# Gated rows finished in their own turn, and two down tiles side by side in PSUM, in the feed-forwards of a two-block network

## The chip, the cores and the metric

One core of a Trainium2 chip runs the whole network in one launch. The metric is the device time in microseconds (us) of one execution. "PE" is TensorE, "DVE" VectorE, "ACT" ScalarE, "POOL" GpSimd and "SP" the queue that issues the weight transfers.

## What is computed

A network of two blocks on 512 positions of width 1024. What matters here are the two convolutional feed-forwards at the end of the second block (`l` = 0 and 1). In outline:

```
y = rmsnorm(h, ffn_norm_g[l])
u = y @ w_up[l]                      # 1024 -> 2 x 2816
u = causal conv of width 3 over positions, per channel, plus bias
g = silu(u[:, :2816]) * u[:, 2816:]  # the gated rows
h = h + g @ w_down[l]                # 2816 -> 1024
```

Everything is kept transposed: a tile has 128 channels on the partitions and the 512 positions along the free axis. Float32 products are made of three TensorE products: each operand is split into a high part of reduced precision and the remainder, and high*high, high*low and low*high are summed in PSUM.

## The kernel before

**Plan.** `Plan` (from line 90) lists every PSUM tile of the program in the order in which TensorE fills them. A tile has 1024 float32 columns; there are four such buffers (`BANKS2`), and each tile takes the next one in the ring, waiting until the tile that was there has been read (`before`, `free`). The plan also lists the 128x128 weight blocks in the order of use, eight to a unit (`UT`).

**Weights.** SP loads a unit from memory into one of five `raw` buffers (line 417). ACT copies it to its high part `whi` (line 814), POOL subtracts to get `wlo` (line 1194); there are three buffers of each. ACT does this inside its own stream: `psum(key)` of ACT (line 818) converts whatever units the plan allows before and, in the feed-forwards, right after the wait for tile `key`. A unit may be converted once the last tile that used the unit three before it is finished.

**Feed-forward** (`ffn`, in `Plan`, and in TensorE's, ACT's and DVE's streams). The 2816 gated channels are made in two halves (`f` = 0, 1) of `FH` = 11 rows of 128 channels. For each row there is one *up tile*: 16 weight blocks, 8 into each 512-column half (the two inputs of the gate), so 48 matmuls. After the 11 up tiles of a half come 8 *down tiles* (`m` = 0 to 7), each 11 weight blocks over the 11 gated rows, so 33 matmuls. With two layers and two halves there are four passages from up tiles to down tiles.

A gated row is made so, once its up tile is finished:

- DVE multiplies the tile by `rstd` (`scaled`, line 1210, 1024 columns);
- ACT writes tap 0 and the bias for each half into `cv` (line 831, twice);
- DVE adds the other two taps to each half (line 1216, four instructions);
- ACT takes Silu of the first half into `tmp` (line 831);
- DVE multiplies it by the second half into `hf` (line 1210);
- ACT copies `hf` to the high part `Fhi` (`high`, line 831);
- DVE subtracts to get `Flo` (`low`, line 1210).

The order is written out by hand. In turn `r` DVE does the scaling and the taps of row `r`, and after that the product of row `r-1`; a `Flo` is only made when a third `hf` is asked for (`to_split`, two buffers) or at the end (`flush`). ACT does tap 0 of row `r`, then Silu of row `r-1`, then the high part of row `r-2`. So a row is spread over three turns. TensorE's `linear` waits before block `k` of a down tile for the `Flo` of row `k` (semaphore `lo`).

After a down tile DVE adds it to `X` (`resid`). For the second half of layer 0 this is done inside `feed`, which also makes the next stage's operand.

Of the kernel before, what the change touches and what calls it, by code (L numbers as in the profile page):

```python
# [90 lines left out]
class Plan:  # L91
# [3 lines left out]
    def __init__(self):  # L95
# [2 lines left out]
        self.last = {}  # L98
        self.slot, self.before, self.in_slot, self.turn = [], [], {}, 0

        def tile(key, free, weights=(), again=None, slots=None):
            self.index[key] = n = len(self.free)
            self.free.append(free)
            slot = (slots or range(BANKS2))[self.turn % len(slots or range(BANKS2))]
            self.turn += 1
            self.slot.append(slot)
            self.before.append(self.in_slot.get(slot))
            self.in_slot[slot] = n
            start = len(self.split)
            if again is not None:  # L110
                start, weights_n = self.first[self.index[again]], self.count[self.index[again]]
            else:
                weights_n = len(weights)
                for w in weights:
                    if len(self.split) % UT == 0:
                        self.units.append(("split", len(self.split) // UT))
                    self.split.append(w)
            self.first.append(start)
            self.count.append(weights_n)
            for i in range(start, start + weights_n):  # L120
                self.last[("split", i // UT)] = len(self.free) - 1
# [131 lines left out]
        def ffn(l):  # L253
            for f in range(2):
                for j in range(FH):
                    tile(("up", l, f, j), [("conv", 4 * ((2 * l + f) * FH + j + 1))],
                         ktiles(f"up{l}", f * FH + j) + ktiles(f"up{l}", 2 * FH + f * FH + j))
                    if f == j == 0:
                        norm(f"ffn{l}")
                for m in range(8):  # L260
                    tile(("dn", l, f, m), [("resid", RAT[f"f{l}{f}"] + m + 1)],
                         [(f"dn{l}", f * FH + k, m) for k in range(FH)])

        ffn(0)
        for m in range(8):
# [40 lines left out]
def hf_of(j):  # L306

    return HAT[f"act{j // (2 * FH)}{j // FH % 2}"] + j % FH + 1


def build(nc, a):
# [23 lines left out]
    with ctx:  # L335
# [62 lines left out]
        def v_(name, i=0, n=1):  # L398
            return vec[:, VAT[name][0] + i:VAT[name][0] + i + n]
# [25 lines left out]
        def _(pe):  # L425
# [326 lines left out]
            def ffn(l):  # L752
                for f in range(2):
                    for j in range(FH):
                        tile(("up", l, f, j))
                        for part in range(2):
                            last = linear(("up", l, f, j), *((Ahi, Alo) if l else (Bhi, Blo)), 0, SAT[f"ffn{l}"] + 1, XO, offset=KD * part,
                                          ks=list(range(KD)), col0=T * part)
                        done(last)
                        if f == j == 0:  # L760
                            norm(f"ffn{l}")
                    for m in range(8):
                        tile(("dn", l, f, m))
                        done(linear(("dn", l, f, m), Fhi, Flo, 0, SAT[f"act{l}{f}"] + 1, XO))

# [20 lines left out]
        def _(ac):  # L786
# [308 lines left out]

            def ffn(l):
                for f in range(2):
                    for r in range(FH + 2):
                        if r < FH:
                            ps = psum(("up", l, f, r))  # L1100
                            if f == r == 0:
                                root(f"ffn{l}")
                            j = (2 * l + f) * FH + r
                            if j >= 3:
                                ac.wait_ge(sem("hf"), hf_of(j - 3))
                            ac.wait_ge(sem("scaled"), j + 1)
                            for part in range(2):
                                c = (part * 2 + f) * FH + r
                                act(cv[:, j % 3, part, :], ps[:, part * T:(part + 1) * T], ACT.Identity,
                                    v_(f"ffn_b{l}", c), v_(f"ffn_w{l}", 88 + c), "ca")  # L1110
                        if 1 <= r <= FH:
                            j = (2 * l + f) * FH + r - 1
                            ac.wait_ge(sem("conv"), 4 * j + 4)
                            act(tmp[:, j % 2, 0:T], cv[:, j % 3, 0, :], ACT.Silu, sem_name="se")
                        if r >= 2:
                            high(Fhi[:, r - 2, :])
                    if f == 0:
                        for m in range(8):
                            psum(("dn", l, f, m))
# [85 lines left out]
        def _(ve):  # L1205
# [3 lines left out]
            def tt(out, x, y, op, s=None):  # L1209
                do(TTi(out, x, y, op), s)  # L1210
# [174 lines left out]
            out(PAIRS - 1, TN - 1)  # L1385
            scales(1)

            def resid(key, m, gate=None, n_sem="resid"):
                ps = psum(key)
                if gate is None:  # L1390
                    tt(X[:, m, :], ps[:, 0:T], X[:, m, :], ADD, n_sem)
                else:
                    stt(X[:, m, :], ps[:, 0:T], gate, X[:, m, :], MUL, ADD, n_sem)

# [249 lines left out]
            def feed(name, gain, end, hi, lo):  # L1644

                i = NI[name]
                ve.wait_ge(sem("psum"), plan.index[("ss", NORMS[i - 1][0])] + 1)

                def ahead(k):
                    ve.wait_ge(sem("ah"), LAT[name] + k + 1)  # L1650
                    stt(lo[:, k, 0:T], X[:, k, :], v_(gain, k), hi[:, k, 0:T].bitcast(fp32), MUL, SUB, "lo")
                    if k:
                        ve.wait_ge(sem("n_sq"), nsq[0] + k + 1)
                        g = NK[i] + k
                        first = sq[:, (g - 1) % 3, 0:T] if k == 1 else acc[:, 0:T]
                        tt(acc[:, 0:T], first, sq[:, g % 3, 0:T], ADD, "n_acc")

                for m in range(8):
                    resid((*end, m), m)
                    if m:  # L1660
                        ahead(m - 1)
                ahead(7)
                nsq[0] += 8

            def used():
                ts(small2[:, 0:1], eps1[:, 0:1], 1.0, None, MUL, s="n_use")
# [6 lines left out]

            def ffn(l):
                for f in range(2):
                    for r_ in range(FH + 1):
                        if r_ < FH:

                            ps = psum(("up", l, f, r_))
                            j = (2 * l + f) * FH + r_  # L1680
                            if f == r_ == 0:
                                ve.wait_ge(sem("n_rs"), 2 * NI[f"ffn{l}"] + 2)
                            scaled(ps, "scaled")
                            if f == 1 and r_ == FH - 1:
                                used()
                            for part in range(2):
                                ve.wait_ge(sem("ca"), 2 * j + part + 1)
                                c = (part * 2 + f) * FH + r_
                                for back in (1, 2):
                                    y = cv[:, j % 3, part, back:T]  # L1690
                                    stt(y, ps[:, part * T:part * T + T - back], v_(f"ffn_w{l}", 44 * (2 - back) + c), y,
                                        MUL, ADD, "conv")
                        if r_:
                            j = (2 * l + f) * FH + r_ - 1
                            ve.wait_ge(sem("se"), j + 1)
                            e = tmp[:, j % 2, 0:T]
                            b = to_split(T)
                            tt(b, e, cv[:, j % 3, 1, :], MUL, "hf")
                            queued(Fhi[:, r_ - 1, :], Flo[:, r_ - 1, :])
                    flush()  # L1700
                    if f == 0:
                        for m in range(8):
                            resid(("dn", l, f, m), m)

            feed("ffn0", "ffn_g0", ("ev",), Bhi, Blo)
            ffn(0)
# [21 lines left out]
            flush()  # L1728
            feed("ffn1", "ffn_g1", ("od",), Ahi, Alo)
            ffn(1)  # L1730
            for m in range(8):
                resid(("dn", 1, 1, m), m)
            sums("f2")
            ve.wait_ge(sem("n_rs"), 2 * NI["f2"] + 2)
            for k in range(KD):
# [121 lines left out]
```

## Time and profile before

| | us |
|---|---|
| median of 3 runs | 2248.68 |
| lowest and highest | 2245.04, 2254.93 |
| the profiled execution's own time | 2256.99 |
| its span in the trace | 2254.8 |
| mean granted TensorE clock | 0.926 of full speed |

The profile is of one execution, 8.3 us above the median of the runs. Spans and starts in its rows are in us from the start of the span, unless marked ns. The feed-forwards and the short convolution mixer between them fill the stretch from about 1293 to 2236 us.

### The profile page before, as it was taken

The page shows a single profiled execution, that of the slowest core. Times are in us where ns is not written, and L with a number is a line of the kernel's source. Part 1 is how long each engine was busy: PE and PEld are TensorE (multiplying, and loading weights), DVE is VectorE, ACT ScalarE, POOL GpSimd, SP SyncE. Part 2 cuts the span into 40 slices and gives each one's busy share as a digit, 9 for nine tenths or more (in the row PEclk, how much of TensorE's full clock was granted, in tenths as well). Part 3 has the DMA queues.
Part 4 walks back from the last instruction along what each step waited for, and adds up shares of the span by engine and source line. Part 5 has one row for each costly group of instructions (what it writes and reads, how often), then busy time and mean ns, then how long its engine had stood idle before and what let it go on. Part 6 is the DMA issues. An engine that isn't in the chain of part 4 may idle for free.

```text
span 2254.8 us, 27585 instructions
## 1 busy us (share of the span) xinstructions
PE 1992.5 (88%) x10708; PEld 1606.3 (71%) x10708; DVE 1171.8 (52%) x1657; ACT 887.4 (39%) x1199; POOL 694.8 (31%) x310
## 2 busy tenths in 40 slices
PE   4899999999787977976683999999999999999996
PEld 3687677777666867764472788788778877878875
DVE  2422666664276757657799334225444464522442
ACT  3252656654334453443331444234432234422432
POOL 1121011102214223222235344344344443444432
PEclk6799999999978989878796999999999999999998
DMA  7111211212211100112120222223223322323331
GB/s 277 38 56 54 76 48 67 76 67 85 59 37 37 39 29 29 38 52 80 37 76 10 84 84 94 88 96 98 84 87 101 93 89 90 94 84 94 94 94 47
DMA packets 46257, 166.80 MB, mean 74 GB/s; under 512 B 5392, under 2 KB 5520, under 8 KB 45872
## 3 DMA queue, kind: packets, MB, share of 16 engines
q1 hardware_dynamic: 44208, 158.88, 22.1%
q10 hardware_dynamic: 1920, 6.16, 0.8%
q8 instruction: 86, 1.41, 0.3%
q14 instruction: 43, 0.35, 0.1%
HBM read 162.92 MB, written 2.10 MB: 73 GB/s over the span
## 4 chain that ended last, share of the span: by engine, by line
PE 75%; DVE 17%; ACT 4%; issue 2%; DMA 1%; POOL 0%; ACTq 0%; DVEq 0%
PE ps L454 20%; PE ps L455 20%; PE ps L456 20%; PE ps L559 4%; PE ps L572 2%; PE ps L589 2%; DVE ex L1210 2%; DVE sq L1210 2%; DVE hf L1210 2%; ACT sq L831 1%; DVE tmp L1210 1%; PE ps L488 1%; DVE acc L1210 1%; PE ps L476 1%; DVE wS L1605 1%
## 5 line engine op out<-in xcount | busy, mean ns | idle before, releaser
L1194 POOL TENSOR_TENSOR wlo<-raw,whi 128x1024 fp32r<-128x1024 f32 x251 | 607.7, 2434 | 1303.8 <-ACT whi L814 1303.8
L814 ACT ACTIVATE whi<-raw 128x1024 fp32r<-128x1024 f32 x251 | 257.7, 1055 | 669.1 <-PE ps L456 647.2
L454 PE MATMUL ps<-Ahi,whi 128*128 128x512 f32 (+1 forms) x784 | 320.1, 408 | 27.5 <-issue 11.9
L455 PE MATMUL ps<-Alo,whi 128*128 128x512 f32 (+1 forms) x784 | 314.9, 402 | 0.0
L456 PE MATMUL ps<-Ahi,wlo 128*128 128x512 f32 (+1 forms) x784 | 313.5, 400 | 0.0
L1210 DVE TENSOR_TENSOR ps<-ps,rstd 128x1024 f32<-128x1024 f32 (+1 forms) x60 | 69.7, 1162 | 263.8 <-PE ps L456 227.3
L454 PEld LDWEIGHTS ps<-Ahi,whi 128*128 128x128 f32 x784 | 154.8, 197 | 72.5 <-issue 23.0
L454 PE MATMUL ps<-Fhi,whi 128*128 128x512 f32 x416 | 167.5, 403 | 13.1 <-DVE Flo L1210 12.9
L456 PEld LDWEIGHTS ps<-Ahi,wlo 128*128 128x128 f32 x784 | 154.6, 197 | 33.7
L455 PEld LDWEIGHTS ps<-Alo,whi 128*128 128x128 f32 x784 | 154.9, 198 | 32.1 <-issue 0.5
L1216 DVE SCALAR_TENSOR_TENSOR cv<-ps,vec,cv 128x511 f32<-128x511 f32 (+1 forms) x176 | 131.9, 749 | 71.6 <-ACT cv L831 66.9
L456 PE MATMUL ps<-Fhi,wlo 128*128 128x512 f32 x416 | 165.9, 399 | 0.0
L455 PE MATMUL ps<-Flo,whi 128*128 128x512 f32 x416 | 165.6, 398 | 0.0
L1210 DVE TENSOR_TENSOR X<-ps,X 128x512 f32<-128x512 f32 x48 | 33.2, 692 | 211.4 <-PE ps L456 211.4
L455 PE MATMUL ps<-Blo,whi 128*128 128x512 f32 x352 | 139.2, 395 | 0.0
L454 PE MATMUL ps<-Bhi,whi 128*128 128x512 f32 x352 | 139.2, 395 | 0.0
L456 PE MATMUL ps<-Bhi,wlo 128*128 128x512 f32 x352 | 138.2, 393 | 0.0
L559 PE MATMUL ps<-K,Q 128*128 128x256 f32 (+1 forms) x320 | 115.0, 474 | 2.2 <-ACT V L831 1.2
L454 PEld LDWEIGHTS ps<-Fhi,whi 128*128 128x128 f32 x416 | 79.4, 191 | 37.8 <-DVE Flo L1210 20.7
L831 ACT ACTIVATE sq<-sq,small 128x768 f32<-128x768 f32 (+1 forms) x96 | 76.2, 794 | 72.5 <-DVE small L1349 72.3
L454 PE MATMUL ps<-Hhi,whi 128*128 128x512 f32 x224 | 80.8, 361 | 14.6 <-issue 9.0
L456 PEld LDWEIGHTS ps<-Fhi,wlo 128*128 128x128 f32 x416 | 79.6, 191 | 17.7
(252 smaller groups left out, 3919.9 us busy)
## 6 DMA issues: line engine op xcount, KB each, us to landing
raw<-in_units SPq DMA_DIRECT2D x299, 512.0 KB, 3.7
X<-in_xT ACTq DMA_DIRECT2D x1, 2048.0 KB, 12.8
out_xT<-X SPq DMA_DIRECT2D x8, 256.0 KB, 2.1
CX<-in_ctxT ACTq DMA_DIRECT2D x1, 1024.0 KB, 15.7
masks<-in_masks ACTq DMA_DIRECT2D x1, 512.0 KB, 3.5
acc<-in_rope ACTq DMA_DIRECT2D x1, 384.0 KB, 3.0
gmw<-in_gmw ACTq DMA_DIRECT2D x1, 384.0 KB, 2.9
bs<-in_bs ACTq DMA_DIRECT2D x1, 384.0 KB, 3.5
```

The costliest lines, as they stand in the source:

```text
L454: nc.tensor.matmul(out, sh, mh, start=first, stop=False)
L455: nc.tensor.matmul(out, sh, ml, start=False, stop=False)
L456: return nc.tensor.matmul(out, sl, mh, start=False, stop=last)
L476: last = nc.tensor.matmul(ps[:, c0:min(n, c0 + T)], ones[:, 0:P], acc[:, c0:min(n, c0 + T)], start=True, stop=True)
L559: last = nc.tensor.matmul(ps[:, o0:o0 + c1 - c0], Q[:, p % 2, i, q * P:(q + 1) * P], K[:, p % 2, i, c0:c1], start=True, stop=True)
L572: last = nc.tensor.matmul(ps[64 * i:64 * i + 64, 0:P], V[:, t, h * HV:(h + 1) * HV], PT[:, i, n * P:(n + 1) * P], start=n == 0, stop=n == ...
L589: last = nc.tensor.transpose(ps[:, n * P:(n + 1) * P], Pr[:, u % 3, n * P:(n + 1) * P], ident[:, :])
L814: nc.scalar.activation(whi[:, s % CONV, :], raw[:, c % RAW, :], ACT.Copy).then_inc(sem("whi"), 1)
L831: do(nc.scalar.activation(out, in_, f, scale=scale, **kw), sem_name)
L1194: nc.gpsimd.tensor_tensor(wlo[:, s % CONV, :], raw[:, plan.unit_at[("split", s)] % RAW, :], whi[:, s % CONV, :].bitcast(fp32), ALU.subtrac ...
L1210: do(TTi(out, x, y, op), s)
L1216: do(STTi(out, x, sc, y, op0, op1), s)
```

## The change

In ACT's and DVE's streams, a row is finished in the turn of its own up tile: ACT does tap 0, waits for the two taps of the first half (not for all four), takes Silu, waits for the product and makes the high part; DVE does scaling and taps, waits for Silu, multiplies, waits for the high part and makes `Flo`.

In the plan and in TensorE's stream, down tiles 0 and 1 share one PSUM buffer, tile 0 in its first 512 columns and tile 1 in its last. TensorE does the blocks of rows 0 to 9 for `m` = 0, those of rows 0 to 9 for `m` = 1, and then row 10 for `m` = 0 and for `m` = 1. The first signal comes after 10 blocks, the second after 12 more; both additions to `X` wait for the second. The weight blocks are stored in this new order. The number of matmuls is the same.

```diff
-        def tile(key, free, weights=(), again=None, slots=None):
+        def tile(key, free, weights=(), again=None, slots=None, beside=None):
...
+            else:
+                slot = self.slot[self.index[beside]]
+                self.before.append(None)
...
+                w = lambda m, ks: [(f"dn{l}", f * FH + k, m) for k in ks]
+                tile(("dn", l, f, 0), [("resid", RAT[f"f{l}{f}"] + 2)], w(0, range(FH - 1)))
+                tile(("dn", l, f, 1), [("resid", RAT[f"f{l}{f}"] + 2)],
+                     w(1, range(FH - 1)) + w(0, [FH - 1]) + w(1, [FH - 1]), beside=("dn", l, f, 0))
+                for m in range(2, 8):
+                    tile(("dn", l, f, m), [("resid", RAT[f"f{l}{f}"] + m + 1)], w(m, range(FH)))
...
-                    for m in range(8):
+                    for m in range(2):
+                        ps = tile(("dn", l, f, m))
+                        for i in range(FH - 1 + 2 * m):
+                            k, o = (i, m) if i < FH - 1 else (FH - 1, i - FH + 1)
+                            pe.wait_ge(sem("lo"), SAT[f"act{l}{f}"] + k + 1)
+                            last = product(ps[:, o * T:(o + 1) * T], tuple(weights(("dn", l, f, m), i)),
+                                           (Fhi[:, k, :], Flo[:, k, :]), k == 0, k == FH - 1)
+                        done(last)
+                    for m in range(2, 8):
...
-                        if 1 <= r <= FH:
-                            j = (2 * l + f) * FH + r - 1
-                            ac.wait_ge(sem("conv"), 4 * j + 4)
-                            act(tmp[:, j % 2, 0:T], cv[:, j % 3, 0, :], ACT.Silu, sem_name="se")
-                        if r >= 2:
-                            high(Fhi[:, r - 2, :])
+                        ac.wait_ge(sem("conv"), 4 * j + 2)
+                        act(tmp[:, j % 2, 0:T], cv[:, j % 3, 0, :], ACT.Silu, sem_name="se")
+                        high(Fhi[:, r, :])
...
-                        if r_:
-                            j = (2 * l + f) * FH + r_ - 1
-                            ve.wait_ge(sem("se"), j + 1)
-                            e = tmp[:, j % 2, 0:T]
-                            b = to_split(T)
-                            tt(b, e, cv[:, j % 3, 1, :], MUL, "hf")
-                            queued(Fhi[:, r_ - 1, :], Flo[:, r_ - 1, :])
-                    flush()
+                        ve.wait_ge(sem("se"), j + 1)
+                        b = to_split(T)
+                        tt(b, tmp[:, j % 2, 0:T], cv[:, j % 3, 1, :], MUL, "hf")
+                        queued(Fhi[:, r_, :], Flo[:, r_, :])
+                        flush()
```

## Rows read from the trace of the kernel before

**Rows 1.** The page, busy time of engines: us, share of span, instructions.
```profile
PE 1992.5 (88%) x10708; PEld 1606.3 (71%) x10708; DVE 1171.8 (52%) x1657; ACT 887.4 (39%) x1199; POOL 694.8 (31%) x310
PE 75%; DVE 17%; ACT 4%; issue 2%; DMA 1%; POOL 0%; ACTq 0%; DVEq 0%
```

**Rows 2.** Waits of PE, 1245 to 2255 us: in total, times, longest.
```profile
PE ps L454 <- DVE Flo L1210: 12.9, 10, 2.8
```

**Rows 3.** The same view, 1790 to 1830 us (mixer's output tiles).
```profile
PE ps L454 <- DVE Flo L1210: 2.8, 1, 2.8
```

**Rows 4.** Windows by stage, up and down in turn: length, busy by engine, PEclk, DMA.
```profile
1305.09:1417.50 112.41, 112.41 (x483) 90.89 (x481) 53.39 (x66) 49.15 (x61) 47.77 (x20) 1.00 0.30 94
1417.50:1482.80 65.30, 62.78 (x265) 50.23 (x264) 13.23 (x18) 15.95 (x18) 26.31 (x11) 0.97 0.29 89
1482.80:1603.66 120.86, 120.86 (x530) 99.16 (x529) 54.06 (x67) 47.28 (x59) 52.61 (x22) 1.00 0.30 96
1603.66:1668.34 64.68, 62.71 (x266) 50.27 (x264) 33.04 (x30) 23.40 (x30) 27.23 (x11) 0.97 0.30 90
1872.42:1982.70 110.28, 110.28 (x482) 90.31 (x481) 53.38 (x66) 49.09 (x61) 47.85 (x20) 1.00 0.31 96
1982.70:2048.05 65.35, 62.39 (x265) 49.55 (x264) 13.23 (x18) 15.93 (x18) 26.27 (x11) 1.00 0.28 89
2048.05:2171.25 123.20, 123.20 (x529) 99.79 (x528) 54.06 (x67) 47.33 (x59) 52.56 (x22) 1.00 0.32 94
2171.25:2235.58 64.33, 61.47 (x265) 49.09 (x263) 13.38 (x19) 14.87 (x17) 23.91 (x10) 1.00 0.14 41
```

**Rows 5.** Timeline of PE, first down tile of the first passage.
```profile
1422.16 0.39 PE L456 MATMUL ps<-Fhi,wlo 128*128 128x512 f32 x1
1424.44 0.50 PE L454 MATMUL ps<-Fhi,whi 128*128 128x512 f32 x1 [1.89 <-DVE Flo L1210]
...
1429.93 0.39 PE L454 MATMUL ps<-Fhi,whi 128*128 128x512 f32 x1
```

**Rows 6.** Timeline of DVE, ACT and POOL, the turn of row 10 there.
```profile
1417.77 1.23 DVE L1210 TENSOR_TENSOR ps<-ps,rstd 128x1024 f32<-128x1024 f32 x1 [3.85 <-PE ps L456]
1420.56 3.10 DVE L1216 SCALAR_TENSOR_TENSOR cv<-ps,vec,cv 128x511 f32<-128x511 f32 x4 [1.56 <-ACT cv L831]
1423.69 0.69 DVE L1210 TENSOR_TENSOR Flo<-hf,Fhi 128x512 fp32r<-128x512 f32 x1
...
1426.60 1.48 DVE L1210 TENSOR_TENSOR Flo<-hf,Fhi 128x512 fp32r<-128x512 f32 x2
...
1417.78 2.01 ACT L814 ACTIVATE whi<-raw 128x1024 fp32r<-128x1024 f32 x2 [6.38 <-PE ps L456]
1419.69 1.57 ACT L831 ACTIVATE cv<-ps,vec 128x512 f32<-128x512 f32 x2
...
1423.76 0.63 ACT L831 ACTIVATE tmp<-cv 128x512 f32<-128x512 f32 x1 [1.16 <-DVE cv L1216]
...
1418.92 4.74 POOL L1194 TENSOR_TENSOR wlo<-raw,whi 128x1024 fp32r<-128x1024 f32 x2 [6.43 <-ACT whi L814]
```

**Rows 7.** Timeline of DVE and ACT, first two rows of layer 1.
```profile
1877.05 1.23 DVE L1210 TENSOR_TENSOR ps<-ps,rstd 128x1024 f32<-128x1024 f32 x1 [10.72 <-ACT rstd L831]
1879.28 3.11 DVE L1216 SCALAR_TENSOR_TENSOR cv<-ps,vec,cv 128x511 f32<-128x511 f32 x4 [1.00 <-ACT cv L831]
1884.09 1.23 DVE L1210 TENSOR_TENSOR ps<-ps,rstd 128x1024 f32<-128x1024 f32 x1 [1.70 <-PE ps L456]
...
1887.61 1.28 ACT L831 ACT_TABLE_LOAD   x1
```

**Rows 8.** Timeline of DVE and POOL, a subtraction beside POOL's.
```profile
1861.77 2.32 DVE L1216 SCALAR_TENSOR_TENSOR Alo<-X,vec,Ahi 128x512 fp32r<-128x512 f32 x1 [1.09 <-ACT Ahi L831]
...
1864.85 0.75 DVE L1216 SCALAR_TENSOR_TENSOR Alo<-X,vec,Ahi 128x512 fp32r<-128x512 f32 x1
...
1861.13 2.41 POOL L1194 TENSOR_TENSOR wlo<-raw,whi 128x1024 fp32r<-128x1024 f32 x1 [3.09 <-ACT whi L814]
```

More of the change, by code:

```diff
@@ L99, in __init__ @@
         self.slot, self.before, self.in_slot, self.turn = [], [], {}, 0
-        def tile(key, free, weights=(), again=None, slots=None):
+        def tile(key, free, weights=(), again=None, slots=None, beside=None):
             self.index[key] = n = len(self.free)
             self.free.append(free)
-            slot = (slots or range(BANKS2))[self.turn % len(slots or range(BANKS2))]
-            self.turn += 1
+            if beside is None:
+                slot = (slots or range(BANKS2))[self.turn % len(slots or range(BANKS2))]
+                self.turn += 1
+                self.before.append(self.in_slot.get(slot))
+            else:
+                slot = self.slot[self.index[beside]]
+                self.before.append(None)
             self.slot.append(slot)
-            self.before.append(self.in_slot.get(slot))
             self.in_slot[slot] = n
@@ L259, in ffn @@
                         norm(f"ffn{l}")
-                for m in range(8):
-                    tile(("dn", l, f, m), [("resid", RAT[f"f{l}{f}"] + m + 1)],
-                         [(f"dn{l}", f * FH + k, m) for k in range(FH)])
+                w = lambda m, ks: [(f"dn{l}", f * FH + k, m) for k in ks]
[4 more added lines that the diff above has]
+                    tile(("dn", l, f, m), [("resid", RAT[f"f{l}{f}"] + m + 1)], w(m, range(FH)))
         ffn(0)
@@ L761, in ffn @@
                             norm(f"ffn{l}")
-                    for m in range(8):
+                    for m in range(2):
[7 more added lines that the diff above has]
+                    for m in range(2, 8):
                         tile(("dn", l, f, m))
@@ L1097, in ffn @@
                 for f in range(2):
[L1098 to L1110, printed above, removed]
-                        if 1 <= r <= FH:
-                            j = (2 * l + f) * FH + r - 1
-                            ac.wait_ge(sem("conv"), 4 * j + 4)
-                            act(tmp[:, j % 2, 0:T], cv[:, j % 3, 0, :], ACT.Silu, sem_name="se")
-                        if r >= 2:
-                            high(Fhi[:, r - 2, :])
+                    for r in range(FH):
+                        ps = psum(("up", l, f, r))
+                        if f == r == 0:
+                            root(f"ffn{l}")
+                        j = (2 * l + f) * FH + r
+                        if j >= 3:
+                            ac.wait_ge(sem("hf"), hf_of(j - 3))
+                        ac.wait_ge(sem("scaled"), j + 1)
+                        for part in range(2):
+                            c = (part * 2 + f) * FH + r
+                            act(cv[:, j % 3, part, :], ps[:, part * T:(part + 1) * T], ACT.Identity,
+                                v_(f"ffn_b{l}", c), v_(f"ffn_w{l}", 88 + c), "ca")
+                        ac.wait_ge(sem("conv"), 4 * j + 2)
+                        act(tmp[:, j % 2, 0:T], cv[:, j % 3, 0, :], ACT.Silu, sem_name="se")
+                        high(Fhi[:, r, :])
                     if f == 0:
@@ L1386, in _, with resid @@
             scales(1)
-            def resid(key, m, gate=None, n_sem="resid"):
+            def resid(key, m, gate=None, n_sem="resid", at=0):
                 ps = psum(key)
                 if gate is None:
-                    tt(X[:, m, :], ps[:, 0:T], X[:, m, :], ADD, n_sem)
+                    tt(X[:, m, :], ps[:, at:at + T], X[:, m, :], ADD, n_sem)
                 else:
@@ L1658, in feed @@
                 for m in range(8):
-                    resid((*end, m), m)
+                    if end[0] == "dn" and m < 2:
+                        resid((*end, 1), m, at=m * T)
+                    else:
+                        resid((*end, m), m)
                     if m:
@@ L1663, in feed, with downs @@
                 nsq[0] += 8
+            def downs(l, f, n):
+                for m in range(n):
+                    resid(("dn", l, f, max(m, 1)), m, at=T if m == 1 else 0)
             def used():
@@ L1675, in ffn @@
                 for f in range(2):
[L1676 to L1692, printed above, removed]
-                        if r_:
-                            j = (2 * l + f) * FH + r_ - 1
-                            ve.wait_ge(sem("se"), j + 1)
-                            e = tmp[:, j % 2, 0:T]
-                            b = to_split(T)
-                            tt(b, e, cv[:, j % 3, 1, :], MUL, "hf")
-                            queued(Fhi[:, r_ - 1, :], Flo[:, r_ - 1, :])
@@ L1700, in ffn @@
-                    flush()
+                    for r_ in range(FH):
+                        ps = psum(("up", l, f, r_))
+                        j = (2 * l + f) * FH + r_
+                        if f == r_ == 0:
+                            ve.wait_ge(sem("n_rs"), 2 * NI[f"ffn{l}"] + 2)
+                        scaled(ps, "scaled")
+                        if f == 1 and r_ == FH - 1:
+                            used()
+                        for part in range(2):
+                            ve.wait_ge(sem("ca"), 2 * j + part + 1)
+                            c = (part * 2 + f) * FH + r_
+                            for back in (1, 2):
+                                y = cv[:, j % 3, part, back:T]
+                                stt(y, ps[:, part * T:part * T + T - back], v_(f"ffn_w{l}", 44 * (2 - back) + c), y,
+                                    MUL, ADD, "conv")
+                        ve.wait_ge(sem("se"), j + 1)
[3 more added lines that the diff above has]
+                        flush()
@@ L1701, in ffn @@
                     if f == 0:
-                        for m in range(8):
-                            resid(("dn", l, f, m), m)
+                        downs(l, f, 8)
             feed("ffn0", "ffn_g0", ("ev",), Bhi, Blo)
@@ L1730, in _ @@
             ffn(1)
-            for m in range(8):
-                resid(("dn", 1, 1, m), m)
+            downs(1, 1, 8)
             sums("f2")
```

## The prediction

> **What bounds the kernel now.** I read the busy times first: TensorE is busy for 88% of the span and takes 75% of the chain that ended last [rows 1]. Then its waits over the feed-forwards: all that it waits there for gated rows is 12.9 us in 10 waits [rows 2], of which 2.8 us lie in the mixer's output tiles, which the change does not touch [rows 3]. So 10.1 us of named waits stand at the four passages from up to down tiles. A wait is not all that a stall costs, so I went by the length of whole stages [rows 4]. The up stretches are free of waits: PE is busy for their whole length. A stretch of 11 up tiles has 11 x 48 = 528 matmuls, one that starts behind the norm tile has 480. That gives the spacing of matmuls in undisturbed work: 112.41/480 = 234.2 ns, 120.86/528 = 228.9, 110.28/480 = 229.8 and 123.20/528 = 233.3. The reader is to see two rhythms there, near 229 and near 233 ns, at the same full granted clock. A down stretch has 8 x 33 = 264 matmuls and takes 65.30, 64.68, 65.35 and 64.33 us, 259.66 us together, though 264 undisturbed matmuls would take 60.4 to 61.8 us. What is above that is the price of the stall.
>
> What makes it is seen in one passage [rows 5, 6]. TensorE starts down tile 0 at 1417.5, does rows 0 to 6 and stops at 1422.16; row 7 comes at 1424.44, because its `Flo` was made only behind the taps of row 10 (at 1423.69). Rows 8, 9 and 10 come one by one, the last `Flo` ends at 1428.08. At 1429.93 the 34th matmul of the stage starts, where 1417.5 + 33 x 0.2333 = 1425.2 was due: 4.7 us lost. The granted clock of that stage is 0.97, in the second down stretch too, and 1.00 in the other two [rows 4]: for some 3 to 4 us after the gap the array ran at the lower level of 1.2 GHz, which is why these two losses are larger than their waits.
>
> **Part 1: a row in its own turn (ACT and DVE).** No instruction is added or removed on either engine; their order and their waits change. Take the turn from the signal of its up tile, 0 = 1417.77 [rows 6]. Scaling: 0 to 1.2. ACT converts two weight units, 0 to 2.0, then tap 0 twice until 3.5. DVE's four taps: 2.8 to 5.9, so the first half has both of its taps at 2.8 + 1.55 = 4.35. New from here: Silu waits for those two only, 4.4 to 5.1, beside the last two taps. The product can start when DVE is through the taps: 5.9 to 6.6. High part 6.7 to 7.3, `Flo` 7.4 to 8.1 (each of the three 0.63 to 0.69 by the rows, 0.07 between engines). So a row is ready 8.1 us after its tile, where row 10 took 10.3 us and row 9 some 21 (its `Flo` is the first of the two from 1426.60, its tile came a turn of 11.2 us before row 10's). A turn lasts as long as TensorE needs for an up tile, 48 x 0.229 = 11.0 us at least. 2.9 us are to spare, so DVE and ACT, which now stand waiting in mid-turn, are back before the next tile's signal. Behind ACT's waits stand the conversions of weights: they come at 0 of each turn, as before. Cost in the up stretches: nothing, covered by those 2.9 us.
>
> The first turn of a layer starts late, since `rstd` must come first: scaling at 1877.05 in layer 1 [rows 7]. First two taps done at 1879.28 + 1.55 = 1880.8, the table load for Silu (1.28) moves into this turn, Silu until 1882.8, then 0.72 each for product, high part and `Flo`: 1885.0. The next tile was scaled at 1884.09, so DVE comes 0.9 us late once; its taps wait for ACT's tap 0, which stands behind 2.0 us of conversions, so little moves. ACT is 0.2 us late: the unit that it converts first is needed 8 blocks x 0.69 = 5.5 us after the signal and is ready after 0.2 + 1.1 + 0.1 + 2.4 = 3.8 us. Cost: nothing, bound 1 us in each layer if the cover fails.
>
> **Part 2: two down tiles side by side (TensorE).** Rows 0 to 9 are ready when TensorE arrives: row 9 at 8.1 us of its turn, which is 3 us before. Row 10 is ready 8.1 us after the start of the down tiles. TensorE now has 20 blocks x 3 x 0.229 = 13.7 us of other work before it. Margin 5.6 us. With part 1 alone row 10 would be asked for after 6.9 us and 1.3 us would stay open. Weights: the unit that holds blocks 24 to 31 may be converted when down tile 0 signals, which comes after 10 blocks, 7.2 us; ACT is through with row 10 at 7.3; 1.06 us of ACT and 2.41 of POOL [rows 8] make it ready near 11, needed at 16.5. The later units hang on tile ends that keep their place among the matmuls. SP loads as before, since no unit's last user moves. The addition to `X` for m = 0 comes with that for m = 1; the next user of their buffer is down tile 5. The ring is still four deep. Cost: nothing.
>
> **The sum.** Four down stretches go from 259.66 us to 4 x 264 undisturbed matmuls. At the quickest spacing (228.9) that is 241.7 us, a gain of 17.9; at the slowest (234.2) 247.3, a gain of 12.4. I take the mean of the four spacings, 231.6 ns, as no row says which rhythm a stage will fall into: 244.5 us, **a gain of 15.1 us**. In the profiled execution, 2256.99 - 15.1 = 2241.9; against the median of the runs 2248.68 - 15.1 = **2233.6 us**. The profiled execution lies 8.3 us above that median; the stalls are set by the order of instructions and should be alike in both.
>
> The unknown is the rhythm of what follows. It changed at the stalls (from 234 to 229 ns over the first passage, from 229.8 to 233.3 over the third), so taking them away may leave a stage in the other one. The up stretch of 120.86 us could take 528 x 0.2342 = 123.7 (+2.8), that of 123.20 could take 120.9 (-2.3) or 123.7 (+0.5). With the bounds above the gain is 12.4 - 3.3 = 9.1 to 17.9 + 2.3 = 20.2 us.
>
> The Trainium skill (TensorE: Matmul & The Clock Gate, part 1) gives one spacing for back-to-back matmuls of 512 columns at full clock, N/2.4 GHz + 2.5 ns = about 216 ns. By that figure the down stretches would fall to 4 x 57 us and the sum would be a gain of 32 us. The up stretches, which never wait, contradict it, and I go by them.
>
> **Rivals.**
>
> *The slow rhythm takes part of the gain.* For it: both changes named lie at stalls that go, and the stage before the first passage is in the slow one. Against it: the stage before the third is in the quick one. All stages from the first passage on at 234.2 ns: gain 9.1, 2239.6 us. Inside 0.5% of the median, which is 11.2 us and about what a measurement of this kernel can tell from no change.
>
> *A new stall in place of the old.* The share of a stall that row 10 or a weight unit could bring back, if the chain of 8.1 us were 14 or more, or POOL came late: half of the gain left, 2241 us. Against it: margins of 5.6 and 5.5 us.
>
> *Slower: the turn does not fit.* DVE and ACT now wait on each other three times in a turn. A DVE subtraction with both inputs in SBUF took 2.32 us where it ran beside POOL's, and 0.75 without [rows 8]. Product and `Flo` are of that kind. If both were held up so, the turn would have 8.1 + 2 x 1.6 = 11.3 us against 11.0, ACT would convert weights 0.3 us later in each turn, and after the 1.7 us to spare there (5.5 - 3.8) TensorE would wait for weights. 44 turns x 0.3 = 13 us would stand against 15 gained. It decides from a chain of 11.0 us on; at 12 us (POOL itself pushed back as well) 44 x 1.0 = 44 us are lost, 2278 us. Against it: POOL's two subtractions end at 1418.92 + 4.74 = 1423.66, just as the taps end, so product and `Flo` fall into POOL's idle time.
>
> The Trainium skill (SBUF — State Buffer, Who interferes with whom) has it that a VectorE instruction with two SBUF inputs and a GpSimd one exclude each other for their whole length. Rows 8 agree. By that rule the product can never start before 5.9 us of a turn, whatever Silu does, and a chain that slips by 4 us would run into the next turn's subtractions.
>
> **How the numbers follow.** Forecast, gain of 11 to 20 us: 0.77. Slow rhythm, 0.14. New stall, 0.06. Turn too long, 0.03. The change does what it says in the code, so no case for that. Faster by over 0.5%: 0.77; within: 0.14 + 0.06 = 0.20; slower: 0.03. Range: the bounds of the gain give 2228.5 to 2239.6; the runs shown lie from 3.6 below to 6.3 above their median. That makes 2225 to 2245, which takes in the second and third cases.
>
> **What would show it.** Right: each down stretch 60.4 to 61.8 us long with granted clock 1.00; TensorE's waits for `Flo` down to the mixer's 2.8 us; ACT waiting some 1.6 us in each turn between Silu and the high part, DVE 0.7 us before each `Flo`; the last `Flo` ending 8.1 us after the last up tile's signal. Part 1 wrong: up stretches over 124 us with waits of TensorE for `wlo`. Part 2 wrong: a wait at the 61st matmul of a down stretch. Wrong as a whole: down stretches as forecast and the time not lower, for then something outside them has grown.

## The result, and the profile after

| | before | changed |
|---|---|---|
| median, us | 2248.17 (8 runs) | 2235.51 (8 runs) |
| lowest and highest | 2245.04, 2255.85 | 2230.99, 2243.45 |
| profiled execution: its time, span | 2256.99, 2254.8 | 2241.67, 2239.3 |

The ratio is 0.9939, with a 95% interval of 0.9916 to 0.9962: 0.6% faster, 12.7 us by the medians. One of the eight runs of the changed kernel took 6806 us; the highest above and the ratio are without it, the median is of all eight (2233.27 without it, 14.9 us less than before). Measured again, the ratio was 0.9937 [0.9916, 0.9957], 16.3 us by the medians.

The windows by stage, of the changed kernel, in the same order as [rows 4]: up and down stretches in turn, with length, busy time of PE, PEld, DVE, ACT and POOL, granted clock, DMA.

```profile
1303.45:1415.85 112.40, 112.40 (x482) 90.88 (x481) 56.14 (x70) 51.15 (x64) 47.77 (x20) 1.00 0.30 94
1415.85:1477.45 61.60, 61.60 (x265) 49.90 (x264) 10.46 (x14) 14.04 (x15) 26.29 (x11) 1.00 0.29 94
1477.45:1600.65 123.20, 123.20 (x529) 99.79 (x528) 56.83 (x71) 49.22 (x62) 52.53 (x22) 1.00 0.30 94
1600.65:1662.25 61.60, 61.60 (x265) 49.90 (x264) 30.28 (x26) 21.51 (x27) 27.25 (x11) 1.00 0.31 94
1861.34:1973.74 112.40, 112.40 (x482) 90.88 (x481) 56.13 (x70) 51.14 (x64) 47.77 (x20) 1.00 0.31 94
1973.74:2035.34 61.60, 61.60 (x266) 49.90 (x264) 10.46 (x14) 14.04 (x15) 26.30 (x11) 1.00 0.29 95
2035.34:2158.54 123.20, 123.20 (x530) 99.79 (x528) 56.83 (x71) 49.22 (x62) 52.54 (x22) 1.00 0.31 94
2158.54:2220.14 61.60, 61.60 (x265) 49.71 (x263) 10.61 (x15) 12.99 (x14) 23.90 (x10) 1.00 0.15 43
```

Every down stretch is 61.60 us and PE is busy in all of it, at full granted clock; before, they were 64.3 to 65.4. But the up stretches show no gain: 466.75 us together before, 471.20 now. All eight stretches run at one spacing here, 61.60/264 = 233.3 ns, the slower of the two rhythms.

The waits of PE over the feed-forwards and the mixer (1245 to 2212 us): in total, times, longest.

```profile
PE ps L461 <- DVE Alo L1227: 3.3, 3, 2.6
PE ps L461 <- DVE Flo L1221: 2.8, 1, 2.8
```

Of 12.9 us for `Flo` [rows 2] the mixer's 2.8 [rows 3] are left. The turn of row 10 at the first passage, timelines of DVE, ACT and POOL, beside [rows 6]:

```profile
1416.13 1.23 DVE L1221 TENSOR_TENSOR ps<-ps,rstd 128x1024 f32<-128x1024 f32 x1 [3.06 <-PE ps L463]
1418.91 3.10 DVE L1227 SCALAR_TENSOR_TENSOR cv<-ps,vec,cv 128x511 f32<-128x511 f32 x4 [1.55 <-ACT cv L846]
1422.05 0.69 DVE L1221 TENSOR_TENSOR hf<-tmp,cv 128x512 f32<-128x512 f32 x1
1423.57 0.69 DVE L1221 TENSOR_TENSOR Flo<-hf,Fhi 128x512 fp32r<-128x512 f32 x1 [0.83 <-ACT Fhi L846]
...
1420.54 0.63 ACT L846 ACTIVATE tmp<-cv 128x512 f32<-128x512 f32 x1 [0.92 <-DVE cv L1227]
1422.84 0.63 ACT L846 ACTIVATE Fhi<-hf 128x512 fp32r<-128x512 f32 x1 [1.66 <-DVE hf L1221]
...
1417.28 4.77 POOL L1205 TENSOR_TENSOR wlo<-raw,whi 128x1024 fp32r<-128x1024 f32 x2 [6.42 <-ACT whi L829]
```

The only `Flo` of the turn ends 1424.26 - 1416.13 = 8.1 us after the signal. The product starts at 1422.05, where POOL's two subtractions end (1417.28 + 4.77) and where DVE's own taps end as well (1418.91 + 3.10), so these rows do not tell which of the two set its start. ACT waits 1.66 us between Silu and the high part, and DVE 0.83 us before `Flo`.

Where the 15.5 us between the two spans went: down stretches 259.66 to 246.40, 13.3 less; up stretches 4.5 more; the stretch between the two layers, with the mixer (1668.34 to 1872.42 before, 1662.25 to 1861.34 now), 204.1 to 199.1, 5.0 less, though nothing in it was changed; all ahead of the first up stretch, 1.6 less; the tail the same. The eight feed-forward stretches alone gave 8.8 us.

The windows tell where the 5.0 us lie. The first mixer tile, the stretch of 528 matmuls behind it and the output stretch, before:

```profile
1668.34:1685.87 17.53, 14.85 (x51) 11.19 (x50) 6.26 (x5) 4.78 (x7) 5.20 (x2) 0.81 0.18 60
1685.87:1809.48 123.61, 123.61 (x531) 99.96 (x529) 55.85 (x46) 40.27 (x48) 56.84 (x23) 1.00 0.29 91
1809.48:1859.71 50.23, 47.45 (x193) 37.80 (x192) 30.63 (x30) 17.21 (x22) 19.84 (x9) 0.93 0.30 92
```

The middle one in the changed kernel (the other two are shown with the last experiment: 16.11 us at 0.89 and 49.00 us at 0.97):

```profile
1678.36:1799.63 121.27, 121.27 (x530) 99.33 (x529) 55.28 (x46) 40.27 (x48) 57.24 (x23) 1.00 0.30 93
```

2.3 us are the rhythm of the 528 matmuls, and 2.6 us lie in the two short stretches with a wait in them, which ran at a higher granted clock in this execution.

### The profile page after: what moved, and what is told of

It reads as the page before. It is cut to its first block, busy times and chain, and to the rows that moved or that the text cites. A ratio compares the mean times of both kernels' runs of the same rounds, so it can differ in the third digit from the quotient of the medians.

```text
span 2239.3 us, 27617 instructions
## 1 busy us (share of the span) xinstructions
PE 1985.8 (89%) x10708; PEld 1602.5 (72%) x10708; DVE 1171.5 (52%) x1657; ACT 887.7 (40%) x1199; POOL 695.7 (31%) x310
## 4 chain that ended last, share of the span: by engine, by line
PE 74%; DVE 18%; ACT 5%; issue 2%; DMA 1%; POOL 0%; ACTq 0%; DVEq 0%
PE ps L461 20%; PE ps L462 20%; PE ps L463 20%; PE ps L566 4%; DVE ex L1221 3%; PE ps L579 2%; PE ps L596 2%; DVE sq L1221 2%; DVE hf L1221 1%; ACT sq L846 1%; DVE tmp L1221 1%; ACT ex L846 1%; PE ps L495 1%; DVE acc L1221 1%; DVE wS L1616 1%
## 6 DMA issues: line engine op xcount, KB each, us to landing
X<-in_xT ACTq DMA_DIRECT2D x1, 2048.0 KB, 12.7
```

## The experiments

**Each part alone.** *Own turn alone*: ACT and DVE of the changed kernel, plan and TensorE of the one before.

```diff
-                    for m in range(2):
-                        ps = tile(("dn", l, f, m))
-                        for i in range(FH - 1 + 2 * m):
...
-                    for m in range(2, 8):
+                    for m in range(8):
                         tile(("dn", l, f, m))
                         done(linear(("dn", l, f, m), Fhi, Flo, 0, SAT[f"act{l}{f}"] + 1, XO))
```

> Only the order on ACT and DVE (a row finished in its own turn); plan, TensorE and down tiles as in the kernel before. Theory (late rows make the stall, each part removes its own share): TensorE asks for row 10 after 10 blocks, 7.0 us after the start of down tile 0, and it is ready 0.3 + 8.1 = 8.4 us after it; one wait of about 1.4 us in each of the four passages, no lower clock level behind it, so a down stretch of 62 to 63.5 us and a gain of some 9 to 10 us on the kernel before (ratio about 0.996). Rival (the gain comes from the side-by-side tiles): stretches near 64.5 us, no gain. Rival (the own turn alone is enough): stretches of 61.6 us and the full 13 to 15 us.

Measured: 2239.58 us, ratio 0.9947 [0.9930, 0.9963]: 12.3 us under the kernel before as measured beside it (2251.83 us), where 9 to 10 were expected; in its profile all stretches run near 229 ns. A down stretch and, in PE's timeline, its one wait:

```profile
1411.87:1474.02 62.15, 60.72 (x266) 49.48 (x264) 10.46 (x14) 14.04 (x15) 26.39 (x11) 1.00 0.30 93
```

```profile
1418.51 0.39 PE L460 MATMUL ps<-Fhi,wlo 128*128 128x512 f32 x1
1420.33 0.50 PE L458 MATMUL ps<-Fhi,whi 128*128 128x512 f32 x1 [1.43 <-DVE Flo L1210]
```

One wait of 1.43 us at each of the four passages, for row 10, and none for rows 7 to 9: as the theory said. The gap in the starts of matmuls is 1.82 us where 0.23 is due, and no lower clock follows it. All four down stretches are 62.14 to 62.15 us in this profile, 1.7 more than 264 matmuls at its own spacing of 228.9 ns.

*Side by side alone*: plan and TensorE of the changed kernel, ACT and DVE of the one before.

```diff
-                    for r in range(FH):
+                    for r in range(FH + 2):
...
-                        ac.wait_ge(sem("conv"), 4 * j + 2)
-                        act(tmp[:, j % 2, 0:T], cv[:, j % 3, 0, :], ACT.Silu, sem_name="se")
-                        high(Fhi[:, r, :])
+                        if 1 <= r <= FH:
+                            j = (2 * l + f) * FH + r - 1
+                            ac.wait_ge(sem("conv"), 4 * j + 4)
+                            act(tmp[:, j % 2, 0:T], cv[:, j % 3, 0, :], ACT.Silu, sem_name="se")
+                        if r >= 2:
+                            high(Fhi[:, r - 2, :])
```

> Only the plan and TensorE (down tiles 0 and 1 in one buffer, row 10 of both last); ACT and DVE keep the order of the kernel before, a row over three turns. Theory: rows 7, 8 and 9 still come at about 6.9, 8.4 and 9.9 us after the start of the down tiles where TensorE wants row 7 at 4.9; row 10 came 0.65 us after row 9, which is one block, so putting it off saves almost nothing: down stretches of 64 to 65 us, gain 0 to 2 us. Rival (row 10 is what the stall is made of): stretches near 61.6 us and a gain over 10 us.

Measured: 2251.69 us, ratio 0.9999 [0.9982, 1.0016]: nothing. PE's timeline at the second passage:

```profile
1606.49 0.50 PE L461 MATMUL ps<-Fhi,whi 128*128 128x512 f32 x1 [1.97 <-DVE Flo L1225]
...
1607.94 0.50 PE L461 MATMUL ps<-Fhi,whi 128*128 128x512 f32 x1 [0.49 <-DVE Flo L1225]
...
1609.40 0.50 PE L461 MATMUL ps<-Fhi,whi 128*128 128x512 f32 x1 [0.48 <-DVE Flo L1225]
```

TensorE stops for row 7 and takes rows 8 and 9 as they come. Row 10, put off, has no wait, but it would have come right behind row 9. Down stretches 64.23 to 65.38 us. So, without the own turn, rows 7 to 9 make the stall. Only the own turn repairs them, and the buffer shared by two tiles is worth something only after that.

**What the second part is worth behind the first.** Both kernels once more, on one chip.

> The changed kernel once more, beside own_turn_again on the same chip. Two questions. Rhythm: if TensorE falls into one of its two spacings anew in each execution, this profile shows again no wait of TensorE at the passages, each down stretch either 60.4 or 61.6 us long, but not necessarily in the same pattern as before (slow to 1670, quick to 1860, slow behind); if the pattern belongs to the program, it is the same again. Time: 12 to 16 us under the kernel before.

> The own turn alone once more. At equal spacing of the matmuls its down stretches were 1.6 to 1.7 us longer each than those without a wait (62.15 against 60.45 us), so the side-by-side tiles should be worth 6 to 7 us; the two medians of the first measurements lay only 2 us apart, each on its own chip and in its own rhythm. Theory: the median here is 3 to 8 us above changed_again. Rival (the side-by-side tiles push TensorE into the slow rhythm and so give their gain back): the medians within 2 us and changed_again with 233 ns in most of its stages.

Measured: changed kernel 2234.93 us (9 runs), own turn alone 2240.22 us (6 runs), 5.3 us apart by the medians; the changed kernel is 16.3 us under the kernel before, just above the expected 12 to 16. Their ratios to the kernel before are 0.9937 [0.9916, 0.9957] and 0.9946 [0.9929, 0.9963]. The difference lies in the expected 3 to 8 us, but the intervals overlap, so the time alone does not prove it. The stages do: 62.15 against 60.45 us per down stretch at equal spacing, 4 x 1.7 = 6.8 us. The profile of the changed kernel in this second execution, windows of the first four stretches:

```profile
1306.76:1417.05 110.29, 110.29 (x482) 90.32 (x481) 56.13 (x70) 51.13 (x64) 47.83 (x20) 1.00 0.30 96
1417.05:1477.48 60.43, 60.43 (x265) 49.58 (x264) 10.46 (x14) 14.04 (x15) 26.37 (x11) 1.00 0.31 96
1477.48:1598.34 120.86, 120.86 (x530) 99.17 (x529) 56.83 (x71) 49.18 (x62) 52.60 (x22) 1.00 0.33 96
1598.34:1658.78 60.44, 60.44 (x265) 49.57 (x264) 30.29 (x26) 21.50 (x27) 27.27 (x11) 1.00 0.31 96
```

It is the same program as in the section above, with the same instructions and no wait in either, and each stage is 1.9% shorter: 228.9 ns per matmul instead of 233.3. The eight stretches together take 704.03 us here and 717.60 there. So the program does not fix the rhythm. What does stays open; the chip is not excluded for this pair, but it does not fix the rhythm alone either, since on the chip of the second measurement the own turn's first up stretch took 112.41 us (233.3 ns) and the changed kernel's 110.29 us (228.9 ns).

**How much room a turn has.** Three, then six, extra instructions in each row's chain, which only write a scratch tile.

```diff
                         ve.wait_ge(sem("se"), j + 1)
+                        for _ in range(3):
+                            tt(sq[:, 0, 0:T], cv[:, j % 3, 1, :], cv[:, j % 3, 1, :], MUL)
                         b = to_split(T)
```

> The changed kernel with three extra DVE instructions (128x512, one scratch tile as output, nothing of the result touched) between Silu and the product of each row: 3 x 0.72 = 2.2 us more in the chain of a turn. Theory (a turn has 2.9 us to spare at 11.0 us, the chain is then 10.3 us): up stretches as in the changed kernel, 112.4 and 123.2 us, down stretches 61.6, time within 0.3% of the changed kernel. Rival (margin is thinner than the sum says): up stretches longer by up to 44 x 1 us and waits of TensorE for wlo.

Measured: 2233.59 us (3 runs), 0.9928 [0.9900, 0.9956]: the changed kernel's time. Windows of the two up stretches of layer 0, and PE's timeline where it waited:

```profile
1306.00:1417.26 111.26, 110.53 (x482) 90.23 (x481) 76.92 (x100) 51.23 (x64) 47.84 (x20) 1.00 0.31 95
...
1477.69:1598.54 120.85, 120.85 (x529) 99.16 (x528) 77.61 (x101) 49.17 (x62) 52.60 (x22) 1.00 0.32 96
```

```profile
1323.78 0.47 PE L461 MATMUL ps<-Bhi,whi 128*128 128x512 f32 x1 [0.73 <-POOL wlo L1205]
```

DVE is busy for 20.8 us more in each up stretch, and it is free but for one wait for weights in the third up tile of a layer. In layer 0 it is explained by ACT, which converts the weights there only behind the high part of the late first row (its high part at 1319.43):

```profile
1320.10 2.01 ACT L829 ACTIVATE whi<-raw 128x1024 fp32r<-128x1024 f32 x2
```

That is the place where the forecast had the least room: the first row of a layer starts late, its chain ends after the next tile's signal, and ACT converts weights late once.

> The same with six extra instructions, 4.3 us more: a chain of 12.4 us against a turn of 11.0 to 11.2. Theory: each turn now lasts about 12.4 to 12.6 us, so up stretches of 11 tiles near 137 us, 44 x 1.3 = some 55 us more than the changed kernel (about 2290 us). Down stretches still 61.6 us, since row 10 is asked for after 14 us. Rival (queues take it up, because only conversions of weights must be in time): much less, under 15 us.

Measured: 2275.35 us (2 runs), 1.0110 [1.0074, 1.0146], 40 us above the changed kernel, where 55 was expected. PE's waits, and DVE's timeline of one turn in the first up stretch:

```profile
PE ps L461 <- POOL wlo L1205: 29.4, 36, 2.9
```

```profile
1407.34 1.23 DVE L1221 TENSOR_TENSOR ps<-ps,rstd 128x1024 f32<-128x1024 f32 x1
1409.55 3.10 DVE L1227 SCALAR_TENSOR_TENSOR cv<-ps,vec,cv 128x511 f32<-128x511 f32 x4 [0.98 <-ACT cv L846]
1412.68 4.32 DVE L1221 TENSOR_TENSOR sq<-cv 128x512 f32<-128x512 f32 x6
1417.04 0.69 DVE L1221 TENSOR_TENSOR hf<-tmp,cv 128x512 f32<-128x512 f32 x1
1418.56 0.69 DVE L1221 TENSOR_TENSOR Flo<-hf,Fhi 128x512 fp32r<-128x512 f32 x1 [0.83 <-ACT Fhi L846]
1419.28 1.23 DVE L1221 TENSOR_TENSOR ps<-ps,rstd 128x1024 f32<-128x1024 f32 x1
```

The mechanism of the "slower" rival is real: with too long a chain TensorE waits for `wlo`, 36 times over the 44 turns, because ACT converts weights late. Its price was too high. A turn lasts 1419.28 - 1407.34 = 11.94 us and not 12.4: when turns follow without a pause, ACT's conversions run beside `Flo` and the scaling, and DVE waits 0.98 us for tap 0 instead of 1.55. And the first turns of each half use up the room there is before any wait appears: the second up stretch of a layer took 127.9 us, 7.1 more than 528 matmuls at 229 ns, and not 11 x 11.94 = 131. The down stretches were not free, as was expected: they took 62.3 to 62.4 us at 1.00 clock, with waits for `wlo` and `Flo` of 0.7 and 0.6 us in the first one.

**Is the slower rhythm the cost of waits?** TensorE waits for `Flo` and its other operand before every block, though after the first tile each of these waits is met.

```diff
-                            last = linear(..., 0, SAT[f"ffn{l}"] + 1, XO, offset=KD * part,
+                            last = linear(..., 0, SAT[f"ffn{l}"] + 1 if f == j == part == 0 else None, XO, offset=KD * part,
...
-                        done(linear(("dn", l, f, m), Fhi, Flo, 0, SAT[f"act{l}{f}"] + 1, XO))
+                        done(linear(("dn", l, f, m), Fhi, Flo, 0, None, XO))
```

> The changed kernel without the waits for Flo and for the operand that are already met by an earlier wait of TensorE (all up tiles but the first half of the first of a layer, down tiles 2 to 7): 2320 or so fewer waits, same work. It asks what the two rhythms of matmuls are. Theory (rhythm is a phase into which TensorE falls at an interruption): both rhythms, 229 and 233 ns, are still seen, time as the changed kernel within 0.4%. Rival (the 233 ns rhythm is the cost of taking waits): all stages without waits at 229 ns or below, 5 to 9 us less.

Measured: 2239.73 us (9 runs), 0.9950 [0.9932, 0.9968]: no better than the changed kernel. Windows of an up stretch in layer 0 and one in layer 1:

```profile
1482.45:1605.65 123.20, 123.20 (x529) 99.79 (x528) 56.84 (x71) 49.22 (x62) 52.50 (x22) 1.00 0.31 94
...
2037.47:2158.32 120.85, 120.85 (x529) 99.17 (x528) 56.84 (x71) 49.20 (x62) 52.72 (x22) 1.00 0.32 96
```

The slow rhythm is there without the waits, so taking them is not its cost. The rival falls.

**The same idea where TensorE still waited.** In the mixer and in the feeds a row was still finished one turn late.

```diff
-            for r in range(10):
-                if r < 8:
+            for r in range(8):
...
-                if r >= 2:
-                    high(Fhi[:, r - 2, :])
+                high(Fhi[:, r, :])
```

(the mixer, in ACT's stream; DVE's likewise, with `flush()` in each turn) and

```diff
                 for m in range(8):
                     psum((*end, m))
-                    if m:
-                        ahead(m - 1)
-                ahead(7)
+                    if end[0] == "dn" and m == 0:
+                        continue
+                    if end[0] == "dn" and m == 1:
+                        ahead(0)
+                    ahead(m)
```

(the feeds, in ACT's stream; in DVE's simply `ahead(m)` behind each `resid`).

> The changed kernel with the mixer's rows alone finished in their own turn. The last row is ready about 4.8 us after the start of the output tiles, where TensorE wants it at 4.9: output stretch 44 to 45 us, 4 to 5 us less than the changed kernel. If POOL's last subtraction holds the chain up, 1 to 2 us of it stay.

> The changed kernel with the feeds alone in their own turn. Last operand tile of the mixer ready about 4.1 to 4.3 us behind the signal (product of X 0.7, conversions first on ACT until 2.7, the subtraction between or behind POOL's two of 2.4 us each), wanted at 4.6: first mixer tile 11.0 to 11.2 us instead of 15.7, 5 to 6 us less than the changed kernel. Rival: POOL's two subtractions follow each other so closely that DVE comes only behind both, at 6.7 us: 2 us of wait stay.

> The changed kernel with the same idea at the places where TensorE still waits: in the mixer of layer 1 each row finished in its own turn (no side-by-side tiles), and in the feeds (X to the next stage's operand) each tile finished in its own turn instead of one tile later. Theory (late rows are what is left): the mixer's output stretch, 49.0 us in the changed kernel, falls to 192 x 0.229 to 0.233 = 44.0 to 44.8; the first tile behind the down tiles of layer 0, 15.7 us, falls to 11.0 to 11.2; the one behind the mixer, 12.3 us, likewise. Together 9 to 11 us less than the changed kernel, 24 less than the kernel before (ratio near 0.989). Rival (POOL holds the subtractions of the feed up, and the wait stays): 4 to 5 us less only.

Measured: mixer alone 2228.91 us (3 runs), 0.9914 [0.9888, 0.9941]; feeds alone 2229.84 us (2 runs), 0.9913 [0.9882, 0.9945]; both **2228.04 us** (6 runs), 0.9898 [0.9877, 0.9920]. The windows of the first mixer tile, of the mixer's output stretch and of the tile behind it, of the changed kernel first:

```profile
1662.25:1678.36 16.11, 13.43 (x52) 10.11 (x50) 6.26 (x5) 4.79 (x7) 5.19 (x2) 0.89 0.22 65
1799.63:1848.63 49.00, 46.16 (x193) 36.76 (x192) 30.74 (x30) 17.22 (x22) 19.96 (x9) 0.97 0.32 97
1848.63:1861.34 12.71, 12.01 (x52) 9.08 (x50) 5.15 (x5) 3.85 (x6) 2.41 (x1) 1.00 0.21 73
```

and of the kernel with both:

```profile
1666.99:1678.65 11.66, 11.66 (x51) 9.29 (x50) 4.86 (x3) 3.42 (x5) 5.24 (x2) 1.00 0.27 90
1799.92:1844.01 44.09, 44.09 (x193) 35.98 (x192) 29.18 (x26) 17.85 (x23) 19.96 (x9) 1.00 0.34 108
1844.01:1855.46 11.45, 11.45 (x52) 9.23 (x50) 3.71 (x3) 2.49 (x4) 2.41 (x1) 1.00 0.25 81
```

77.8 us became 67.2, that is 10.6 less, within the 9 to 11 expected of the stages. From 1252 to 2207 us its profile shows no wait of TensorE at all. The medians say less, 7 to 7.5 us under the changed kernel, and 22.4 us under the kernel before where 24 were expected. The two single edits cannot be told from the pair by time, with two and three runs each and rhythms of their own; the stages can. With the mixer's edit alone the output stretch took 44.11 us and the two tiles stayed at 16.32 and 12.70; with the feeds' alone each of the two tiles took 11.45 us and the output stretch stayed at 50.25. The kernel with both has the lowest median of this study.

## Why the prediction was right, point by point

- *What bounds the kernel, and what the stall is made of*: right. Undisturbed down stretches were forecast at 60.4 to 61.8 us, and were 61.60 in the first profile and 60.44 in the second.
- *Part 1, the turn*: chain of 8.1 us forecast, 8.1 found; product at POOL's end, as forecast. With 2.2 us more TensorE waited only once in each layer, with 4.3 more in most turns. The room of 2.9 us is bracketed by that.
- *The first turn of a layer*: costed at nothing, and so it was. That this is the tightest place is shown by the run with three extra instructions.
- *Part 2*: a remainder of 1.3 us without it was forecast, and 1.43 us of wait found; with it none. "Without part 1 it would bring nothing" was not said in the prediction; it was expected and shown in the run of its own.
- *The sum*: forecast 15.1 us; the medians give 12.7 us (14.9 without the long run) and 16.3 us in the second measurement, and 2235.5 and 2234.9 against 2233.6 us. What the mechanism gives is read from the down stretches: 259.66 - 246.40 = 13.3 us in the first profile, where all ran slow, and 259.66 - 241.75 = 17.9 us in the second, where all ran quick. These are the two ends of the sum. Taking the mean of four spacings was no better founded than either. The slow end itself was set too low, at 12.4: the 234.2 and 229.8 ns come from stretches behind a norm tile, and hold some 0.4 us of that tile's interruption; the matmuls there ran at 233.3 and 228.9 ns. The bound on the up stretches was too narrow as well. I let only two of them change rhythm (+3.3 or -2.3 us); in fact a third did too (110.28 to 112.40), and with it the up stretches took 4.5 us more.
- *Where it was luck*: in the first pair of profiles the eight stretches gave 259.66 + 466.75 - 717.60 = 8.8 us, under the lowest gain of 9.1 that the sum allowed. That the pair came to 15.5 us, so near the forecast, is due to 6.7 us outside of them, which the prediction did not have: the rhythm and the clock of the mixer (5.0) and what lies ahead of the first up stretch (1.6).
- *Rivals*: the slow rhythm was there and took part of the gain in the feed-forwards, just as that rival describes it; that it is no effect of the change is shown by the second profile, where it is absent. The new stall did not come. The turn that does not fit was made with six extra instructions and behaves as described, at three quarters of the price expected of it (40 us in place of 55). The rival's rule that the product can never start before POOL's pair has ended is too strict: the last section shows a DVE subtraction that got in between two of POOL's.
- *The lower clock* behind the stalls, 0.97 in two of four down stretches [rows 4], is 1.00 in all eight stretches now. The prediction took it for the reason why these two stalls cost more than their waits. It is only a part: in layer 0 the stretches lost 4.8 and 4.2 us (65.30 and 64.68 against some 60.5) with 2.4 and 2.0 us of named waits, but in layer 1, at 1.00, they lost 3.8 and 3.9 us (65.35 - 61.60, 64.33 - 60.44) with waits of 3.0 and 2.9 us. So gaps of the same size brought the lower clock in one layer and not in the other, and the gaps of 1.8 us of the own turn alone brought it in none of the eight passages of its two profiles. The Trainium skill (TensorE: Matmul & The Clock Gate, part 1) names idle time of the array as what brings the lower clock back; the changed kernel, with no gap in the eight stretches and 1.00 in all of them, agrees. The spacing of some 216 ns that the same part gives for back-to-back matmuls of this size is seen in no run: 228.9 and 233.3 ns are.

## What to carry to other kernels

When an engine makes the operands of a later stage in a software pipeline, the depth of the pipeline is paid for at the end of the stage: the last rows all come late together, and the consumer runs into the first of them, not into the last. If the whole chain of a row fits into the producer's turn, finish it there; reordering the consumer pays only for what is then left. And look for the same pattern at every passage: here the mixer and the feeds, by the length of their stages, were worth 10.6 us more, where the four passages that the change repaired gave 13 to 18 us.

## What the runs showed of the hardware

- Uninterrupted streams of these matmuls (128x128 by 512 columns, each with its weight load) run at one of two spacings, 228.9 or 233.3 ns, at the same full granted clock, for hundreds of microseconds. The program being the same, one execution had 704.03 us and another 717.60 us for the same eight stretches, neither with a wait of TensorE in them. In the profiles of the changed kernels the spacing changed at norm tiles, whose single matmul has other operands, and at interruptions; it did not need the semaphore waits between matmuls. What decides it stays open. Since 1.9% of these stretches is 13.6 us, it is as large as the whole gain. It is also of the size of the spread of 6 to 19 us between the runs of one kernel (those with six runs or more); that it makes this spread is not shown, since only one run of each has a profile.
- With two POOL subtractions back to back, a DVE subtraction with both inputs in SBUF took 1.39 us (0.75 without POOL, 2.32 beside a single one: [rows 8]), and the DVE addition behind it 2.74 us in place of 0.69, ending 0.56 us after POOL's second. So the first got in between POOL's two and the second was held until the end of them; this is inferred from the times, as the row gives POOL's two as one. In the feed of the changed kernel this is the timeline of DVE and POOL at its last tile:

```profile
1665.26 1.39 DVE L1227 SCALAR_TENSOR_TENSOR Alo<-X,vec,Ahi 128x512 fp32r<-128x512 f32 x1 [2.04 <-ACT Ahi L846]
1666.68 2.74 DVE L1221 TENSOR_TENSOR acc<-acc,sq 128x512 f32<-128x512 f32 x1
1669.45 0.75 DVE L1227 SCALAR_TENSOR_TENSOR Alo<-X,vec,Ahi 128x512 fp32r<-128x512 f32 x1
...
1663.67 5.19 POOL L1205 TENSOR_TENSOR wlo<-raw,whi 128x1024 fp32r<-128x1024 f32 x2 [5.30 <-ACT whi L829]
```

That addition stood between the last two subtractions of the feed, and TensorE waited 2.6 us for the last of them. With the feeds in their own turn (the run with that edit alone) the other subtraction has been made a tile before, the last one takes the place between POOL's two, and TensorE does not wait; the addition behind it is as slow as before, but nobody waits for it:

```profile
1658.77 1.38 DVE L1229 SCALAR_TENSOR_TENSOR Alo<-X,vec,Ahi 128x512 fp32r<-128x512 f32 x1 [2.04 <-ACT Ahi L846]
1660.19 2.79 DVE L1223 TENSOR_TENSOR acc<-acc,sq 128x512 f32<-128x512 f32 x1
```
